# Normalised rows of seven token tiles and of the MLP tiles transposed by the DMA crossbar instead of the tensor engine

## The reference

```python
h   = x + concat[MLA(n), POOL(n)] @ w_out          # n = rmsnorm(x); proj = n @ w_in
h   = h + square(relu(rmsnorm(h) @ w_mlp_up)) @ w_mlp_down
out = rmsnorm(h)
```

## Time and profile before

| | |
|---|---|
| runs | 1553.7, 1556.51, 1578.97 us; median 1556.51 us |
| profiled execution | 1558.64 us; span of its slowest core, core 5, 1557.1 us |
| spans of the 8 cores | 1548.2 to 1557.1 us |
| mean granted PE clock | 0.984 to 0.988 |
| PE, ACT, DVE, POOL busy | 95%, 38%, 37%, 25% of the span |
| first phase / second phase on core 5 | 0 to 653 us / 653 to 1557 us |

### The profile page before, as it was taken

One profiled execution on the slowest core, in us unless ns is written; L12 is line 12 of the kernel. 1 busy time (PEld: TensorE's weight loads), 2 busy tenths in 40 slices (PEclk: granted clock), 3 DMA queues, 4 the chain that ended last, 5 costly groups with the idle time before them and its releaser, 6 DMA issues.

```text
span 1557.1 us, 23154 instructions; the slowest of 8 cores (1548.2 to 1557.1 us)
## 1 busy us (share of the span) xinstructions
PE 1477.7 (95%) x7484; PEld 660.4 (42%) x7484; DVE 578.1 (37%) x872; ACT 593.9 (38%) x1149; POOL 383.4 (25%) x403
## 2 busy tenths in 40 slices
PE   5858999999999998999999999999999999999998
PEld 2323434344334433344444444444444444444443
DVE  5743636254636433223313323323233233233222
ACT  5645556565545555332222322322322312412212
POOL 2643435142607150012012112111101211210210
PEclk9989999999999999999999999999999999999999
DMA  9668475647665437570200200200200200201001
GB/s 293 175 134 150 124 148 124 119 109 119 148 154 67 124 109 215 162 273 1 109 1 1 108 1 1 108 1 15 95 1 17 92 0 28 82 1 41 15 1 54
DMA packets 44068, 137.07 MB, mean 88 GB/s; under 512 B 4528, under 2 KB 4528, under 8 KB 43568
## 3 DMA queue, kind: packets, MB, share of 16 engines
q1 hardware_dynamic: 31808, 106.18, 21.6%
q0 software_dynamic: 12000, 29.36, 11.9%
q10 hardware_dynamic: 144, 0.05, 0.0%
HBM read 118.28 MB, written 51.38 MB: 109 GB/s over the span
## 4 chain that ended last, share of the span: by engine, by line
PE 87%; DMA 5%; DVE 3%; ACT 2%; issue 2%; SPq 0%; DVEq 0%; ACTq 0%
PE pm L323 86%; ACT arena L329 2%; PE pm L326 2%; DMA arena<-x 1%; DMA arena<-wout 1%; DMA out<-arena 1%; DVE arena L332 1%; DVE arena L341 1%; DMA arena<-cs_tab 0%; DVE arena L347 0%; SPq L353 0%; DVE arena L335 0%; ACT arena L393 0%; DVEq L125 0%; ACT L329 0%
## 5 line engine op out<-in xcount | busy, mean ns | idle before, releaser
L323 PE MATMUL pm<-arena 128*128 128x512 bf16 (+5 forms) x6968 | 1448.3, 376 | 43.8 <-DVE arena L332 19.6
L323 PEld LDWEIGHTS pm<-arena 128*128 128x128 bf16 (+3 forms) x6968 | 627.6, 98 | 850.4 <-issue 163.0
L329 ACT ACTIVATE arena<-pm 128x512 bf16<-128x512 f32 (+4 forms) x768 | 406.7, 572 | 715.0 <-PE pm L323 666.8
L332 POOL TENSOR_TENSOR arena<-arena 128x512 bf16<-128x512 f32 (+6 forms) x248 | 283.4, 1143 | 765.4 <-ACT arena L329 742.3
L332 DVE TENSOR_TENSOR arena<-pm,arena 128x512 f32<-128x512 f32 (+2 forms) x288 | 197.0, 690 | 460.4 <-PE pm L323 382.3
L332 DVE TENSOR_TENSOR arena<-arena 128x512 bf16<-128x512 f32 (+3 forms) x355 | 190.5, 553 | 417.2 <-ACT arena L329 411.4
L329 ACT ACTIVATE arena<-arena 128x1 f32<-128x1 f32 (+5 forms) x202 | 106.7, 535 | 221.4 <-DVE arena L332 191.0
L335 DVE SCALAR_TENSOR_TENSOR arena<-arena 128x1024 bf16<-128x1024 f32 (+1 forms) x64 | 81.8, 1307 | 67.7 <-ACT arena L329 67.7
L393 ACT ACTIVATE arena<-arena 128x1024 bf16<-128x1024 f32 x64 | 67.7, 1058 | 20.4 <-DMA arena<-out 11.9
L347 POOL COPY arena<-arena 128x16 f32<-128x16 f32 x48 | 15.7, 327 | 234.4 <-ACT arena L329 234.4
L326 PE MATMUL pm<-arena 128*128 128x128 bf16 x516 | 39.2, 230 | 28.5 <-DVE arena L341 19.5
(11 more groups left out here) (16 smaller groups left out, 31.5 us busy)
## 6 DMA issues: line engine op xcount, KB each, us to landing
arena<-x SPq DMA_DIRECT2D x64, 512.0 KB, 4.6
out<-arena SPq DMA_DIRECT2D x64, 512.0 KB, 3.0
arena<-out SPq DMA_DIRECT2D x28, 512.0 KB, 5.8
wup_bf<-w_mlp_up POOLq DMA_DIRECT2D x16, 512.0 KB, 14.2
wdn_bf<-w_mlp_down POOLq DMA_DIRECT2D x16, 512.0 KB, 13.3
arena<-wup_bf POOLq DMA_DIRECT2D x8, 1024.0 KB, 8.9
arena<-wdn_bf SPq DMA_DIRECT2D x8, 1024.0 KB, 17.6
arena<-cs_tab SPq DMA_DIRECT2D x28, 128.0 KB, 8.3
```

Of the source, the lines that this page charges most:

```text
L323: return S.add("pe", lambda e: e.matmul(out, lhsT=lhsT, rhs=rhs, start=start, stop=stop, skip_group_check=skip), reads, writes)
L329: return S.add("act", lambda e: e.activation(out=out, in_=in_, func=func, **kw), reads, writes, extra=extra)
L332: return S.add(eng, lambda e: e.tensor_tensor(out=out, in0=in0, in1=in1, op=op), reads, writes, extra=extra)
```

## The change

`norm_trd` takes the place of `norm_tr` for tiles 1 to 7 in the first phase and for all 8 tiles of the second. It is one DMA on SP's queue that transposes a normalised block of 128 x 1024 from xn straight into its place in xnT. Tile 0 keeps the PE path. The weights of t0 to t3 in the filler go from 3 (6 in the last attention tile) to 0, which moves other pieces against the attention steps.

```diff
+    def norm_trd(b):
+        xb, xr_ = NR[0][b % len(NR[0])]
+        S.add("sp", lambda e: e.dma_start_transpose(out=xnT[:, :, b * P:(b + 1) * P], in_=xb), [xr_], [("xnT", b)], dma=True)
@@ N_chunks
         def trn(b):
-            norm_tr(b)
+            norm_trd(b)
             if b == 0:
                 norm_scale(xt, XT_N, 0, 3)
             if b == 1 and t + 1 < NT:
                 load_x(t + 1)
-            d["t%d" % b] = (3, lambda b=b: trn(b))
+            d["t%d" % b] = (0, lambda b=b: trn(b))
@@ last attention tile
-            fl += bulk + nb + [(6, lambda b=b: norm_tr(b)) for b in range(4)]
+            fl += bulk + nb + [(0, lambda b=b: norm_trd(b)) for b in range(4)]
```

## The result

The changed kernel takes **1621 us** where the kernel before takes 1556 us: the ratio is 1.043, with an interval of 1.033 to 1.053, so it is slower. In some executions of either kernel the cores of one die run at a lower clock; the comparisons here leave those out, and of the experiment that moves the x loads one execution is left, and the trace of another is read on its undisturbed die. The forecast was 1546 us with a range of 1526 to 1590, so it was wrong, and on the wrong side.

A forecast was written before the change was run, and what follows sets the result against it. PE was taken as the bound, busy 1477.7 of 1557.1 us. From the profiled 1558.6 us, gains of 25.1 came off and losses of 10 (stalls) and 2.5 (start) were added: 1546 us, range 1526 to 1590.

The forecast's parts named there:

- MLP phase, -12.5 us: MLP phase: seven groups of 32 PE transposes, 1.78 us each, leave PE, a gain of 12.5 us.
- its cover: MLP phase: four transposes at 5 us, 20 us, hide behind the down half's 27.6 us; breaks at 6.9 us each.
- the rotary table's time, tile by tile, where they are crowded, since the transposes will stand in that table's place in the queue: Attention phase: the last two transposes of a tile land as rotary loads do, in 6.5 to 14.7 us.
- The term of 10 us for stalls: Attention tiles 1 to 5: PE waits in front of c0, 2 us a tile, 10 us lost, bounds 0 to 6 a tile.
- the prediction's own sign of being wrong: Attention phase: the forecast is wrong if PE's wait in front of c0 exceeds 5 us a tile.
- Start, 2.5 us lost: Start, tile 1's transposes: two stand behind four x loads and w_out loads come later; 2.5 us lost (4 gained to 6 lost).
- Attention, -10.8 us: Attention phase: 24 blocks of tiles 2 to 7, 0.45 us of PE transposes each, leave PE, a gain of 10.8 us.
- The crowded crossbar: Attention phase: last two transposes wait out staging traffic, land in 20.9 us; c0 stalls, 61 us lost, 1597 us; chance 0.11.
- x loads in the same place take 4.9 us: Attention phase: landing time of x loads, 4.9 us, given as the argument against slow transposes in the crowd.
- The slow crossbar everywhere: Both phases: a transpose takes 8.6 us even with idle DMA engines, MLP phase loses 71 us, 1668 us; chance 0.04.
- The case in which all is hidden: Attention phase and start: c0 never waits, start loses nothing, 9.5 us of idle time and half clock go; 1524 us; chance 0.07.
- The sign that DVE would not be held: Attention phase: DVE's scaling of block 3 does not wait for the first transpose; no cost up to about 6.5 us.

## Why the prediction was wrong

**MLP phase, -12.5 us:** right, 12.2 measured; so was its cover. A transpose landed in 3.3 us (median), not 5, against the 6.9 us where the cover ends. Both rules that the prediction names can now be judged. The Trainium skill, "VectorE: DVE Perf Modes", The three transpose paths, has 1309 ns a block, an estimate of 10.5 us a transpose; the trace says 3.3, and it decides. The Trainium skill's other rule, "as fast as regular DMAs" ("Advanced Engine Details and Errata", X-Bar Transpose), is nearer, with plain stores of the same bytes at 2.4 us.

**The step that failed: "the rotary table's time, tile by tile, where they are crowded, since the transposes will stand in that table's place in the queue".** It took a landing time of another DMA as the price of a new one. The share of 0.87 said that the engines were nearly full for that stretch, and the landing times read there were those of a stretch without the transposes, which bring 1 MB a tile into it. In the attention of tile 1 the last two landed in 23.4 us on the slowest core and not in 8.6, and the table, now behind them, in 18.0. The term of 10 us for stalls became 116.0 - 37.9 = 78.1 us of waits on the slowest core, 7.0 on the fastest. Four of the five stalls there are over 15 us, where the prediction's own sign of being wrong was 5 us a tile.

**Start, 2.5 us lost:** the same error, 15.7 us. The last transpose landed 33 us after its issue, and putting the x loads behind them cut PE's wait from 37.9 to 7.9 us.

**Attention, -10.8 us:** the work did leave PE, but with the casts in place no run with the transposes of tiles 2 to 6 gained it in its time. Where PE hardly waited for a transpose, VectorE waited for rows. Without the casts, behind the fold, 3 to 6 us came, and the start took as much or more.

**The rivals.** The crowded crossbar, 0.11, is what happened: slower, by stalls in front of c0. Its 1597 us came from a landing of 20.9 us and from a start that loses 2.5; the landing was 23.4 here, the start 15.7, the half clock 1.7 us a stall and not 3.4. It deserved the larger chance: "x loads in the same place take 4.9 us" was the argument against it, and those loads stand ahead of the crowd, not in it. The slow crossbar everywhere is refuted by the 3.3 us. The case in which all is hidden needed a c0 that never waits. The sign that DVE would not be held came out: the scaling of block 3 waited for a transpose 1.8 us at most on any core.

**Open:** how much the crossbar costs in the crowd beyond its bytes; and why the same program finds a stretch two to three and a half times slower on one core than on another. Eight cores run it at the same time, and which one is slowest changes from run to run; whether they get in each other's way in memory was not tried.

## What to carry to other kernels

Before work is moved onto DMA, read the DMA share of the very stretch it goes into. At 0.13 the move was free and gave its whole gain; at 0.87 it cost more than it saved, in each of the four orders of transposes, x loads and casts that were run. Price an added DMA there first as bytes on a full resource and ask what lands later, not by the landing time of a neighbour. Split such a change by phase and keep the part that has room.

## What the runs showed of the hardware

- A crossbar transpose of 128 x 1024 bf16 landed 3.3 us after its issue with idle DMA engines (median), at 1.2 us of issue each on SP. In the crowd of tile 1's attention two of them held SP for 16.2 us on core 1, and the rotary loads behind them on its queue went out only then.
- Beside three casts of 512 KB from HBM to HBM, started just before, four 256 KB DMAs of SP landed in 7.2 us (transposes) and 8.6 us (stores, in pieces of 2 KB or of 256 bytes), instead of 3.2, 2.4 and 3.6.
- 28 stores of 256 KB that nobody waits for cost 28 us, in and around the stretch of the tile where the DMA share was 0.87 before.
